# Pair products of two linear-attention mixers written across the partition halves, and small work moved from VectorE to ScalarE

## What is computed

```
x = x + 0.5 * SwiGLU_1(RMSNorm(x))
P = RMSNorm(x) @ w_in          # one projection, columns for 4 head groups
o = concat[RWKV7(P), RGLRU(P), GatedDeltaNet(P), GLA(P)]
x = x + o @ w_out
x = x + 0.5 * SwiGLU_2(RMSNorm(x))
```

## Time and profile before

| | |
|---|---|
| median of 3 runs | 1352.57 us |
| profiled execution, whole | 1353.87 us |
| its span | 1352.1 us |
| TensorE matmul busy | 1329.3 us, 98% |
| TensorE weight loads busy | 1289.2 us, 95% |
| VectorE busy | 855.8 us, 63% |
| ScalarE busy | 692.6 us, 51% |
| GpSimd busy | 77.4 us, 6% |
| DMA | 185.90 MB, mean 137 GB/s |

### The profile page before, as it was taken

How to read it: one execution, slowest core, us unless ns; L and a number is a source line. 1 busy time by engine, 2 the same in 40 slices (tenths; PEclk the granted TensorE clock), 3 DMA queues, 4 the chain that set the end, 5 groups by cost and what they waited for, 6 DMA issues and landing times.

```text
span 1352.1 us, 31424 instructions
## 1 busy us (share of the span) xinstructions
PE 1329.3 (98%) x12584; PEld 1289.2 (95%) x12584; DVE 855.8 (63%) x1327; ACT 692.6 (51%) x995; POOL 77.4 (6%) x113
## 2 busy tenths in 40 slices
PE   7999999999999999999999999999999999999997
PEld 7999999998988999999999999999888899999997
DVE  6656533898876756553376565349988766555533
ACT  7444423757655644443364444347466655454423
POOL 0000000200030100000010000001001310000001
PEclk9999999999999999999999999999999999999999
DMA  8544454322313644444454444443223244444541
GB/s 302 173 143 150 144 155 155 111 79 80 112 50 111 212 145 150 146 154 154 142 189 153 155 143 152 151 144 110 80 79 97 66 158 156 155 148 147 155 142 53
DMA packets 50768, 185.90 MB, mean 137 GB/s; under 512 B 5760, under 2 KB 6272, under 8 KB 50176
## 3 DMA queue, kind: packets, MB, share of 16 engines
q1 hardware_dynamic: 49104, 177.37, 41.3%
q10 hardware_dynamic: 1584, 7.35, 1.5%
HBM read 180.14 MB, written 4.56 MB: 137 GB/s over the span
## 4 chain that ended last, share of the span: by engine, by line
PE 86%; DVE 11%; issue 2%; ACT 1%; DMA 0%; DVEq 0%; ACTq 0%
PE ps L479 27%; PE ps L481 26%; PE ps L480 26%; DVE wl L1592 2%; DVE ar L1749 2%; PE ps L847 1%; DVE ar L1663 1%; PE ps L749 1%; PE ps L1035 0%; DVE raw L1967 0%; PE ps L817 0%; PE ps L1013 0%; PE ps L799 0%; DVE ar L1740 0%; DVE ar L1683 0%
## 5 line engine op out<-in xcount | busy, mean ns | idle before, releaser
L479 PE MATMUL ps<-xh,wh 128*128 128x320 f32 x1952 | 611.8, 313 | 9.0 <-DVE xl L1614 8.0
L1592 DVE TENSOR_TENSOR wl<-raw,wh 128x1024 fp32r<-128x1024 f32 x332 | 408.1, 1231 | 317.5 <-ACT wh L1186 317.1
L481 PE MATMUL ps<-xh,wl 128*128 128x320 f32 x1952 | 604.4, 310 | 0.0
L480 PE MATMUL ps<-xl,wh 128*128 128x320 f32 x1952 | 604.3, 310 | 0.0
L1186 ACT ACTIVATE wh<-raw 128x1024 fp32r<-128x1024 f32 x332 | 349.3, 1054 | 356.2 <-PE ps L481 339.1
L479 PEld LDWEIGHTS ps<-xh,wh 128*128 128x128 f32 x1952 | 367.5, 188 | 20.1 <-issue 9.0
L480 PEld LDWEIGHTS ps<-xl,wh 128*128 128x128 f32 x1952 | 367.7, 188 | 0.5
L481 PEld LDWEIGHTS ps<-xh,wl 128*128 128x128 f32 x1952 | 367.6, 188 | 0.0
L479 PE MATMUL ps<-hid_h,wh 128*128 (+1 forms) x704 | 217.5, 309 | 0.0
L480 PE MATMUL ps<-hid_l,wh 128*128 (+1 forms) x704 | 217.5, 309 | 0.0
L481 PE MATMUL ps<-hid_h,wl 128*128 (+1 forms) x704 | 217.5, 309 | 0.0
(11 more groups left out here) (290 smaller groups left out, 934.6 us busy)
## 6 DMA issues: line engine op xcount, KB each, us to landing
raw<-wts SPq DMA_DIRECT2D x332, 512.0 KB, 3.5
ms<-mst ACTq DMA_DIRECT2D x2, 1440.0 KB, 7.9
mout<-ms ACTq DMA_DIRECT2D x2, 1440.0 KB, 6.6
x<-xT SPq DMA_DIRECT2D x4, 320.0 KB, 4.9
yT<-x SPq DMA_DIRECT2D x4, 320.0 KB, 2.4
cs<-cst SPq DMA_DIRECT2D x1, 652.0 KB, 8.1
pr<-par ACTq DMA_DIRECT2D x1, 429.0 KB, 4.2
pr<-par ACTq DMA_DIRECT2D x1, 425.0 KB, 5.3
```

The costliest lines, as they stand in the source:

```text
L479: pe.matmul(out, a, rh, start=start, stop=False)
L480: pe.matmul(out, a, rl, start=False, stop=False)
L481: return pe.matmul(out, b, rh, start=False, stop=stop)
L1592: tt(wl[:, s, :], raw_of(layer, n), wh[:, s, :].bitcast(F32), ALU.subtract).then_inc(lo_ready.sem, 1)
```

## The change

The second head pair of the pair products is written to the other half of the partitions (`crossed`), with one bank for each pair. ScalarE copies its banks back into BE, CD and KQ (`pairs_home`, `kq_home`), and VectorE masks or decays those parts in place. ScalarE also takes the first tap of GDN's convolution (`first_tap`), the scale of `kk` (folded in its square) and the affine part of the keys (`ka_mix`); the sign of `kk` moves. The orders of ScalarE and VectorE differ as the last hunks show. Waits and signals are renamed to fit (not shown).

```diff
put(ins, "rk_sum")
-def products(src, rhs, three_banks, name):
+def crossed(src, rhs, banks_of, at=None):
     def f(c, p, b):
-        return pe.matmul(ps[half[b], three_banks[c // 2], ((c % 2) * 2 + p) * 128:][:, 0:128],
-                         cht(src, c, p, b), rhs[half[b], c, p].rearrange("q k t -> q (k t)"),
-                         start=True, stop=True)
-    put(each(f), name)
+        to = (c if at is None else at) * 128
+        return pe.matmul(ps[half[b ^ p], banks_of[p], to:to + 128], cht(src, c, p, b),
+                         rhs[half[b], c, p].rearrange("q k t -> q (k t)"), start=True, stop=True)
+    return each(f, range(DEC) if at is None else (DEC,))
...
     on(pe, layer, "rw_gc")
     on(pe, layer, "kk_rn")
-    products(bPi, kkr, (2, 3, 6), "rw_pairs")
-    products(kPi, kkr, (4, 5, 7), "rw_pairs")
+    put(crossed(bPi, kkr, (2, 3)), "rw_pairs")
+    put(crossed(kPi, kkr, (4, 5)), "rw_pairs")
+    crossed(bPi, kkr, (6, 7), 0)
+    put(crossed(kPi, kkr, (6, 7), 1), "rw_pairs")
...
-    products(cq[:, 2:4], kq, (5, 6, 7), "KQ_mm")
+    put(crossed(cq[:, 2:4], kq, (5, 6)), "KQ_mm")
+    put(crossed(cq[:, 2:4], kq, (7, 4), 0), "KQ_mm")
...
+    def pairs_home():
+        for g, (dst, main) in enumerate(((BE, 3), (CD, 5))):
+            on(act, layer, "rw_pairs", g + 1)
+            for b in range(2):
+                say(act.activation(dst[half[b], 0:DEC, 1].rearrange("q c k t -> q c (k t)"),
+                                   ps[half[1 - b], main, :].rearrange("q (c t) -> q c t", c=DEC), ACT.Copy), "pairs_home")
+        on(act, layer, "rw_pairs")
+        for g, dst in enumerate((BE, CD)):
+            for p in range(2):
+                for to, at in pieces(p):
+                    say(act.activation(dst[to, DEC, p].rearrange("q k t -> q (k t)"),
+                                       ps[at, 6 + p, 128 * g:128 * g + 128], ACT.Copy), "pairs_home")
+    def kq_home(last):
+        on(act, layer, "KQ_mm", last + 1)
+        for b in range(2):
+            dst, src = (KQ[half[b], DEC, 1].rearrange("q k t -> q (k t)"), ps[half[1 - b], 4, 0:128]) if last else \
+                (KQ[half[b], 0:DEC, 1].rearrange("q c k t -> q c (k t)"), ps[half[1 - b], 6, :].rearrange("q (c t) -> q c t", c=DEC))
+            say(act.activation(dst, src, ACT.Copy), "kq_home")
...
+    def first_tap(j):
+        act.wait_ge(in_read.sem, in_read.upto(layer, T_GDN + j + 1))
+        on(act, layer, "pads" if j < 3 else "bPi" if j < 5 else "rk_sum")
+        say(act.activation(cv[:, j, 0:CVP - 3], gcp[:, j, 0:CVP - 3], ACT.Copy, scale=P("gcw", j)), "tap0")
...
+    act.wait_ge(S["xm"].sem, S["xm"].upto(layer, 3))
+    for p in range(2):
+        say(act.activation(rsq[:, p, :], xm[:, 2 + p, :], ACT.Square, scale=P("kk", p)), "kk_sq")
     act.preload_act_table_set("natural_log_exp_and_others")
     st(act.activation(tiny[R, 10:11], P("alog")[R], ACT.Exp))
     st(act.activation(lnt[R, :], small[R, :], ACT.Abs, bias=P("dtb")[R]))
     st(act.activation(tiny[:, 11:13], P("lam", 0, 2), ACT.Abs))
-    ahead(5)
     act.wait_ge(S["cum"].sem, S["cum"].upto(layer))
     st(act.activation(rP[:], cum[:], ACT.Exp, scale=-WDEC))
     st(act.activation(Pinv[:], cum[:], ACT.Exp, scale=WDEC))
+    on(act, layer, "ra")
+    on(act, layer, "ka_rest")
+    for p in range(2):
+        say(act.activation(kmod[:, p, :], ra[:, p, :], ACT.Identity, scale=P("ka", p), bias=tiny[:, 13 + p:14 + p]), "ka_mix")
     act.wait_ge(S["prev"].sem, S["prev"].upto(layer))
     say(act.activation(Pprev[:], sg[:], ACT.Exp, scale=-WDEC), "rw_P")
     act.wait_ge(S["kk_sum"].sem, S["kk_sum"].upto(layer))
     log_sums(rsq, 2)
     say(act.activation(rsq[:], rsq[:], ACT.Exp, scale=-0.5), "kk_rn")
+    ahead(5)
     ahead(6)
     ahead(7)
     on(act, layer, "gla_z")
...
     say(act.activation(tiny[:, 11:13], tiny[:, 11:13], ACT.Ln, bias=C("one")), "sp_lam")
     say(act.activation(ltm, ltm, ACT.Ln, bias=C("one")), "gla_ln")
     ahead(8)
+    first_tap(0)
+    pairs_home()
     ahead(9)
+    eye(0)
     ahead(10)
-    eye(0)
     on(act, layer, "rw_rows_mm", 1)
     rows_of(rVt, 2, "rw_rows")
     on(act, layer, "rw_rows_mm", 2)
     home(kLt, 4, "rw_rows")
     on(act, layer, "rw_rows_mm", 3)
     home(bLt, 6, "rw_rows")
+    first_tap(1)
+    inverse_t(0, 1)
+    across(0, 1)
+    first_tap(2)
     act.wait_ge(S["Gb_mm"].sem, S["Gb_mm"].upto(layer))
     for p in range(2):
         say(act.activation(Gb[:, p, :], ps[:, 6 + p, 0:TOK], ACT.Copy), "Gb")
     ahead(11)
-    inverse_t(0, 1)
-    across(0, 1)
     on(act, layer, "Gb")
     say(act.activation(eG[:], Gb[:], ACT.Exp), "eG")
     ahead(12)
+    first_tap(3)
+    first_tap(4)
     ahead(13)
+    first_tap(5)
     across(0, 2)
     inverse_t(0, 2)
...
     say(act.activation(kq[:, :, :, 1, :], chunked(cq[:, 0:2, :]), ACT.Copy), "kq_q")
     ahead(17)
+    kq_home(0)
     inverse_t(0, 5)
+    kq_home(1)
     ahead(18)
     ahead(19)
     across(1, 1)
...
-    def rw_keys_raw():
-        for p in range(2):
-            say(ts(kk[:, p, :], xm[:, 2 + p, :], P("kk", p), -1.0, ALU.mult, ALU.mult), "kkraw")
+    def rw_keys_rest():
+        say(ts(tiny[:, 13:15], P("ka", 0, 2), -1.0, 1.0, ALU.mult, ALU.add), "ka_rest")
     def rw_keys():
-        st(ts(tiny[:, 13:15], P("ka", 0, 2), -1.0, 1.0, ALU.mult, ALU.add))
-        on(ve, layer, "ra")
-        st.settle()
-        for p in range(2):
-            st(ts(kmod[:, p, :], ra[:, p, :], P("ka", p), tiny[:, 13 + p:14 + p], ALU.mult, ALU.add))
-        st.settle()
+        on(ve, layer, "ka_mix")
         st(tt(kmod[:], kmod[:], xm[:, 2:4, :], ALU.mult))
...
-        st(tt(kk[:], kk[:], rsq[:], ALU.mult))
+        for p in range(2):
+            st(stt(kk[:, p, :], xm[:, 2 + p, :], P("kk", p), rsq[:, p, :], ALU.mult, ALU.mult))
         st.settle()
         say(tt(ra[:], kk[:], ra[:], ALU.mult), "rb")
         on(ve, layer, "rw_P")
-        st(tt(kkr[:, :, :, 0, :], chunked(kk), chunked(Pprev), ALU.mult))
+        for p in range(2):
+            st(stt(kkr[:, :, p, 0, :], kk[:, p, :].rearrange("q (c t) -> q c t", c=NC), -1.0,
+                   Pprev[:, p, :].rearrange("q (c t) -> q c t", c=NC), ALU.mult, ALU.mult))
         on(ve, layer, "rb")
-        say(stt(bPi[:], ra[:], -1.0, Pinv[:], ALU.mult, ALU.mult), "bPi")
+        say(tt(bPi[:], ra[:], Pinv[:], ALU.mult), "bPi")
...
-        for g, (src_banks, dst) in enumerate((((2, 3, 6), BE), ((4, 5, 7), CD))):
+        every, short = (tri[:, d].rearrange("q k t -> q (k t)") for d in range(2))
+        for g, (dst, bank) in enumerate(((BE, 2), (CD, 4))):
             on(ve, layer, "rw_pairs", g + 1)
-            for j, bank in enumerate(src_banks):
-                n = 4 if j < 2 else 2
-                say(tt(dst[:, 2 * j:2 * j + n // 2].rearrange("q c p k t -> q (c p) (k t)"),
-                       ps[:, bank, 0:n * 128].rearrange("q (u t) -> q u t", u=n),
-                       tri[:, j // 2].rearrange("q k t -> q (k t)").unsqueeze(1).broadcast_to([128, n, 128]),
-                       ALU.mult), "rw_pairs_read")
+            say(tt(dst[:, 0:DEC, 0].rearrange("q c k t -> q c (k t)"), ps[:, bank, :].rearrange("q (c t) -> q c t", c=DEC),
+                   every.unsqueeze(1).broadcast_to([128, DEC, 128]), ALU.mult), "rw_pairs_read")
+        for g, dst in enumerate((BE, CD)):
+            on(ve, layer, "pairs_home", 2 * g + 2)
+            there = dst[:, 0:DEC, 1].rearrange("q c k t -> q c (k t)")
+            say(tt(there, there, every.unsqueeze(1).broadcast_to([128, DEC, 128]), ALU.mult), "rw_pairs_read")
+        for g, dst in enumerate((BE, CD)):
+            on(ve, layer, "pairs_home", 3 * g + 7)
+            there = dst[:, DEC].rearrange("q p k t -> q p (k t)")
+            say(tt(there, there, short.unsqueeze(1).broadcast_to([128, 2, 128]), ALU.mult), "rw_pairs_read")
...
     def gdn_conv(j):
         on(ve, layer, "shift_kept")
-        for k in range(CONV):
-            st.settle()
+        on(ve, layer, "tap0", j + 1)
+        for k in range(1, CONV):
+            if k > 1:
+                st.settle()
             ins = tap(cv, gcp, j, 6, k, "gcw")
             say(ins, "conv") if k == CONV - 1 else st(ins)
...
+        on(ve, layer, "E")
+        def decayed(cs, p, src):
+            dst, e_ = KQ[:, cs, p], E[:, cs, p, :].unsqueeze(2)
+            say(tt(dst, dst if src is None else src.rearrange("q (c k t) -> q c k t", k=2, t=CH),
+                   e_.broadcast_to(list(dst.shape)), ALU.mult), "KQ")
+        on(ve, layer, "KQ_mm", 1)
+        decayed(slice(0, DEC), 0, ps[:, 5, :])
         on(ve, layer, "KQ_mm")
-        on(ve, layer, "E")
-        for j, bank in enumerate((5, 6, 7)):
-            n = 4 if j < 2 else 2
-            e_ = E[:, 2 * j:2 * j + n // 2].rearrange("q c p t -> q (c p) t").unsqueeze(2).broadcast_to([128, n, 2, CH])
-            say(tt(KQ[:, 2 * j:2 * j + n // 2].rearrange("q c p k t -> q (c p) k t"),
```

(43 more changed lines are left out.)

## The result

The changed kernel takes 1366.92 us (median of 4 runs, 1365.05 to 1367.31), the kernel before 1353.11 us beside it: a ratio of 1.010, 95% interval 1.0086 to 1.0114. It is 13.8 us slower, where I forecast no change. The profiled execution took 1365.05 us with a span of 1363.3, so the two profiles differ by 11.2 us.

A forecast was written before the change was run, and what follows sets the result against it. TensorE bounds the kernel, with VectorE leading from 258 to 328 us. Per layer +2.0 - 0.85 - 1.2 = -0.05 us, twice -0.1, gives 1352.5 us; 8-in-10 range 1348.0 to 1356.5.

The forecast's parts named there:

- The products on TensorE: Crossed 128-column matmuls take 28 ns instead of 58; rw_products save 2.3 us and gdn_products 1.2 us a layer.
- The wait in tile 9: TensorE idles 1.8 us in tile 9 for VectorE's later low split, losing 1.8 of the 2.3 us saved.
- The masks: VectorE's six mask instructions, two waiting shortly for ScalarE's copies, take 3.3 us, from 284.4 to 287.7.
- the layer's +2.0: TensorE starts the first inverse_t 2.0 us later than before, through gla_floor, splits, masks, eye(0) and rows.
- my bounds of 1.6 to 2.6: Range in us for the first inverse_t's delay: masks without waiting, to ScalarE copies at the long end.
- The wait in front of the first inverse: TensorE idles 2.4 us before inverse_t(0, 1), waiting for ScalarE's row copies.
- "twice" in the sum: The layer's sum of -0.05 us was counted for both layers, giving -0.1 us.
- Behind it: After inverse_t(0, 1), vanished waits cut the delay from 2.0 to 1.15 us; GDN's products take off 1.2 us.
- The two old waits: TensorE's waits of 0.35 and 0.5 us behind inverse_t(0, 1), forecast to vanish.
- GDN's copies had cover: kq_home has cover: KQ is complete at about 342.4 us, and gdn_rows needs it at 345.4.
- The chance of the clock: New idle times of 1.8 and 2.4 us may let TensorE's clock fall; priced only as rival 2, chance 0.21.
- rival 2: Slower by the clock: falls behind the new idle times in both layers add 2 x 1.6 us, 1355.7; chance 0.21.

The follow-up runs named there:

- before_two_moves: Kernel before, with the split of tile 9 behind kk_rn and rw_rest and eye(0) ahead of ScalarE's split of tile 14: 1357.19 us, ratio 1.0029.
- split9_early: Changed kernel with the split of tile 9 back at its old place on ScalarE and VectorE: 1361.15 us.
- uncrossed: Changed kernel with the products written to the half they are read from, everything else kept: 1369.11 us.
- split12_early: Changed kernel with the tile 9 split and eye(0) moves undone, and VectorE's splits of tiles 11 and 12 back in front of the masks: 1352.85 us.

## Why the prediction was wrong

**The products on TensorE: right.** 2.35 us from the start of the first products to the next tile (282.69 to 285.04) over 80 matmuls is 29 ns each, forecast 28; the second ones take 1.32 us against 2.40, a saving of 1.1, forecast 1.2. The Trainium skill's rule of about 81 ns per matmul at 128 columns ("TensorE: Matmul & The Clock Gate", "Back-to-back issue gap") does not hold for these 64 x 64 products, with 29 ns crossed and 58 ns uncrossed; the measurement decides.

**The wait in tile 9: right.** 1.94 us, forecast 1.8, and the cause is confirmed by doing and undoing the move (before_two_moves, split9_early).

**The masks: mis-sized.** This is the term of the layer's +2.0 that was too small. VectorE's masks after, with ScalarE's copies:

```profile
284.37 1.29 DVE L1781 TENSOR_TENSOR ar<-ps,cs 128x512 f32<-128x512 f32 x2
285.57 1.47 DVE L1786 TENSOR_TENSOR ar<-ar,cs 128x512 f32<-128x512 f32 x2
287.24 0.43 DVE L1790 TENSOR_TENSOR ar<-ar,cs 128x256 f32<-128x256 f32 x1 [0.21 <-ACT ar L1305]
288.14 0.43 DVE L1790 TENSOR_TENSOR ar<-ar,cs 128x256 f32<-128x256 f32 x1 [0.47 <-ACT ar L1305]
```

```profile
283.86 1.21 ACT L1299 ACTIVATE ar<-ps 64x512 f32<-64x512 f32 x2 [2.15 <-PE ps L659]
...
286.33 1.77 ACT L1305 ACTIVATE ar<-ps 128x128 f32<-128x128 f32 x6
```

They take from 284.37 to 288.48, 4.1 us instead of 3.3. ScalarE's ten copies run from 283.86 to 288.1 instead of 283.5 to 287.3: their starts are a full duration apart, where I let them overlap, and they begin 0.4 us later. With 0.3 us more behind the masks the first `inverse_t` was 3.07 us late, outside my bounds of 1.6 to 2.6. I had also written that what the products saved makes no difference to its start. It does: in uncrossed the copies and the masks wait for the products, and it starts 1.6 us later still (301.40 against 299.81).

**The wait in front of the first inverse: right in place and size** (2.37 us, forecast 2.4), in layer 0. That it holds for both layers was wrong: "twice" in the sum skipped the raw tiles. I had followed the moved splits past VectorE's and ScalarE's queues, not past SyncE's, whose load of tile 14 waits for the split of tile 12 in layer 1. In the changed kernel ScalarE waits 1.3 us for it. With the other two moves undone it was 7.5 us of ScalarE's time, and moving the split brought 5.6 us.

**Behind it: right.** The two old waits vanished, in split12_early too, whose profile has no fall of the clock, and GDN's copies had cover but for 0.3 us (`inverse_t` at level 5 waits for L2024).

**The chance of the clock: the step that failed.** The sum took the clock as unchanged, and rival 2 got 0.21, with one fall a layer at 1.6 us. The rival was the case, and bigger: 20.6 us at the lower level instead of 3.4, in three stretches of 6.9, 3.4 and 10.3 us, where I had priced two of about 3.3. A fall also makes what follows late: the products in layer 1 lie in a low stretch, take 3.26 us instead of 2.41, and delay the copies, the masks and the inverse. Why two of the stretches were so much longer than the one before stays open. The row for it was in the trace of before: a fall behind 0.5 us of idle time. I used it for a rival's price, not for a term of the sum, though I had worked out two new idle times of 1.8 and 2.4 us. The Trainium skill's statement that activity releases the throttle and idleness lets it return ("TensorE: Matmul & The Clock Gate", "What's actually happening") agrees with both filled kernels: no fall where the idle time was filled, 6.7 us at the lower level behind the 1.4 us that stayed.

How the 13.8 us divide can be told only roughly, because schedule and clock feed each other: 8.6 of the 11.2 us between the profiles are half-rate time. The mean clock of all runs says about the same: 0.990 to 0.992 for the changed kernel, 0.997 to 0.999 for the kernel before, and 0.007 of 1366 us is 9.6 of the 13.8. The other 2.6 us are of the size of what the sum left out in the schedule (the first `inverse_t` 1.1 us later in each layer, the load 1.3); no run has them without the clock. The experiments show what each order move is worth together with the falls that it causes: 5.8 us for the split of tile 9, 9.6 for the splits of tiles 11 and 12, 1.1 for `eye(0)`, each undone alone. Which pattern of idle time and small matmuls brings a fall stays open: split12_early, the same code each time, had no fall in its profiled run (mean clock 0.999), and its other runs go down to a mean clock of 0.993.

## What to carry to other kernels

When work is moved between engines in a kernel with one dense engine, sum the new idle times of the dense engine, and price each with the clock fall that it may bring, not with its length alone (here falls stood behind idle times of 0.5 to 4.3 us, though not behind each). Follow a moved step to the loads whose slot it frees, for each turn of the ring apart: two layers of the same code can wait for different tiles. A cheaper product pays as far as the order around it brings its consumers forward: of 6.4 us on TensorE 2.2 arrived in one order and 3.8 in another. The change as a whole lost 13.8 us in the first and gained 5.5 in the second.

## What the runs showed of the hardware

TensorE's 64 x 64 matmuls of 128 columns ran at 29 ns each, counted as the trace counts them, when all four quarters of the array were in use, and at 56 to 58 ns with two. ScalarE's copies from PSUM of 64 partitions by 512 took 0.60 us each, as long a step as their duration. Seven more matmuls a layer made a kernel 7 us faster: they kept the granted clock at 1.00 in layer 0 and took the time at the lower level from 20.6 to 6.7 us.
